# The output gate's vector of an encoder step: summed on ScalarE and GpSimd during the Q, K and V projections, instead of on TensorE inside the recurrent stage

## What is computed

```python
mod = jax.nn.silu(c) @ w_mod + b_mod                 # (1024) @ (1024, 3072)
shift, scale, gate = jnp.split(mod, 3, axis=-1)
hn = rms_norm(x, g_norm) * (1.0 + scale[:, None]) + shift[:, None]
u = hn @ w_in                                        # (T, 1024) @ (1024, 5192)
xa, za, q, k, v, zb, iq, ik, iw = jnp.split(u, IN_OFFSETS, axis=-1)
# A: causal conv of xa, then a gated linear recurrence over the positions (8 blocks of 128 channels)
ya = rms_norm(h.astype(dt), g_a) * jax.nn.silu(za)
# B: index scores pick the top keys of each query; softmax attention over them
yb = rms_norm(ob.astype(dt), g_b) * jax.nn.silu(zb)
y = jnp.concatenate([ya, yb], axis=-1) @ w_out
x_out = x + gate[:, None] * y
```

## Time and profile before

| | us |
|---|---|
| median of 3 runs | 1117.14 (1110.64 to 1118.58) |
| the profiled execution, its own time | 1114.59 |
| its span in the trace | 1112.8 |
| PE busy (5914 matmuls) | 1042.3, 94% |
| DVE busy | 839.2, 75% |
| ACT busy | 497.5, 45% |
| POOL busy | 380.3, 34% |

### The profile page before, as it was taken

One profiled execution on the slowest core, in us unless ns is written; L12 is line 12 of the kernel. 1 busy time (PEld: TensorE's weight loads), 2 busy tenths in 40 slices (PEclk: granted clock), 3 DMA queues, 4 the chain that ended last, 5 costly groups with the idle time before them and its releaser, 6 DMA issues.

```text
span 1112.8 us, 16575 instructions
## 1 busy us (share of the span) xinstructions
PE 1042.3 (94%) x5914; PEld 935.0 (84%) x5914; DVE 839.2 (75%) x1643; ACT 497.5 (45%) x827; POOL 380.3 (34%) x247
## 2 busy tenths in 40 slices
PE   6989898999999999999999997989899899999995
PEld 3679766799999999999999996778788778888873
DVE  1577699999998899999999995667766646543345
ACT  4432365421122677777764235566655524111111
POOL 0122366421111355555557462144231332212120
PEclk9989899999999999999999998999999999999998
DMA  9612001133234122222223432233331337233221
GB/s 298 198 43 67 19 1 40 40 99 96 79 99 109 55 81 81 81 81 69 76 77 101 153 122 87 62 90 96 95 95 29 96 95 236 59 112 100 80 67 57
DMA packets 128280, 100.78 MB, mean 91 GB/s; under 512 B 12176, under 2 KB 119200, under 8 KB 128224
## 3 DMA queue, kind: packets, MB, share of 16 engines
q1 hardware_dynamic: 128224, 100.04, 30.3%
HBM read 74.04 MB, written 25.99 MB: 90 GB/s over the span
## 4 chain that ended last, share of the span: by engine, by line
PE 56%; DVE 23%; issue 13%; ACT 4%; DMA 1%; SPq 1%; POOL 1%; DVEq 0%; ACTq 0%
PE ps L554 16%; PE ps L556 15%; PE ps L555 15%; DVE scores L1984 6%; PE ps L1704 5%; DVE best L1980 5%; DVE hidden L2028 2%; DVE conv L2006 2%; PE ps L1439 2%; DVE scores L1944 1%; PE ps L1424 1%; DVE mult L2023 1%; DMA q_raw<-q_scratch 1%; PE ps L1534 1%; DMA x_in<-in_x_prompt 1%
## 5 line engine op out<-in xcount | busy, mean ns | idle before, releaser
L554 PE MATMUL ps<-h_hi,w_hi 128*128 128x364 f32 (+1 forms) x984 | 327.1, 332 | 4.8 <-DVE h_lo L1882 4.1
L555 PE MATMUL ps<-h_lo,w_hi 128*128 128x364 f32 (+1 forms) x984 | 325.5, 331 | 0.0
L556 PE MATMUL ps<-h_hi,w_lo 128*128 128x364 f32 (+1 forms) x984 | 325.2, 331 | 0.0
L876 POOL TENSOR_TENSOR w_lo<-w_raw,w_hi 128x1024 fp32r<-128x1024 f32 (+1 forms) x41 | 101.2, 2470 | 317.5 <-ACT w_hi L1069 235.3
L554 PEld LDWEIGHTS ps<-h_hi,w_hi 128*128 128x128 f32 (+1 forms) x984 | 185.8, 189 | 6.5 <-issue 4.2
L555 PEld LDWEIGHTS ps<-h_lo,w_hi 128*128 128x128 f32 (+1 forms) x984 | 186.1, 189 | 1.5
L556 PEld LDWEIGHTS ps<-h_hi,w_lo 128*128 128x128 f32 (+1 forms) x984 | 185.4, 188 | 0.7
L1984 DVE MATCH_REPLACE8 scores<-best,scores 128x512 f32<-128x512 f32 (+6 forms) x204 | 172.3, 857 | 0.0
L1980 DVE MAX8 best<-scores 128x8 f32<-128x512 f32 (+6 forms) x204 | 162.8, 860 | 1.8
L1084 ACT ACTIVATE stage<-ps 128x364 f32<-128x364 f32 (+1 forms) x66 | 29.8, 475 | 141.6 <-PE ps L556 133.7
L988 POOL TENSOR_TENSOR y_lo<-y_raw,y_hi 128x1024 fp32r<-128x1024 f32 (+1 forms) x18 | 41.3, 2295 | 142.3 <-ACT y_hi L1341 142.3
(11 more groups left out here) (246 smaller groups left out, 2078.0 us busy)
## 6 DMA issues: line engine op xcount, KB each, us to landing
w_raw<-in_w_in SPq DMA_DIRECT2D x40, 512.0 KB, 4.6
w_mod_raw<-in_w_mod SPq DMA_DIRECT2D x8, 1024.0 KB, 12.6
y_raw<-y_scratch SPq DMA_DIRECT2D x16, 512.0 KB, 4.3
wo_raw<-in_w_out SPq DMA_DIRECT2D x10, 512.0 KB, 4.9
q_scratch<-stage SPq DMA_DIRECT2D x8, 546.0 KB, 3.6
y_scratch<-y_a SPq DMA_DIRECT2D x8, 546.0 KB, 3.5
zb_scratch<-stage SPq DMA_DIRECT2D x8, 546.0 KB, 4.1
x_in<-in_x_prompt SPq DMA_DIRECT2D x8, 512.0 KB, 8.2
```

The source lines that it names most:

```text
L554: nc.tensor.matmul(out, w_part_hi, x_hi, start=first, stop=False)
L555: nc.tensor.matmul(out, w_part_hi, x_lo, start=False, stop=False)
L556: return nc.tensor.matmul(out, w_part_lo, x_hi, start=False, stop=last)
L876: pool.tensor_tensor(w_lo[:, slot, :, 0:width], w_raw[:, slot, :, 0:width], f32(w_hi[:, slot, :, 0:width]), ALU.subtract).then_inc(w_lo_do ...
```

## The change

The last third of `w_mod` is summed elsewhere and earlier. ScalarE issues four loads of 1 MB behind the index stage. Behind each of eight sets of the Q, K and V projections it scales one block of rows by `silu(c)`, once for each of the two vectors, into `wg_part`; GpSimd adds this onto `wg_sum`. Between the first set of the recurrent stage and its loop, TensorE sums `wg_sum` over the partitions with 16 matmuls against a column of ones. The loads and the matmuls inside the loop go. `wg_raw` now has 1024 columns in each of its eight rows and lies over tiles of the recurrent stage, so ScalarE waits for the last add before that stage. The loops over the Q sets are written out on ScalarE and GpSimd.

```diff
-    wg_raw = z.take("wg_raw", [P, KT, P], F32)
+    wg_part = z.take("wg_part", [P, 2, D], F32)
+    wg_sum = z.take("wg_sum", [P, 2, D], F32)
+
+    wg_raw = at("wg_raw", [P, KT, D], F32, zone_x + 4 * nbytes([P, TP + 4], F32))
...
-            def load_gate_block(i):
-
-                if not isinstance(i, int) or i > 0:
-                    sp.wait_ge(gate_ready, i)
-                sp.dma_start(wg_raw[:, :, :], w_mod[:, :, bass.ds(i * P + 2 * D, P)]).then_inc(wg_in, 16)
...
+            def add_gate(k):
+
+                for b in range(2):
+                    pool.wait_ge(wg_scaled, 2 * k + b + 1)
+                    if k >= 1:
+                        pool.wait_ge(wg_added, 2 * k + b - 1)
+                        pool.tensor_tensor(wg_sum[:, b, :], wg_sum[:, b, :], wg_part[:, b, :], ALU.add).then_inc(wg_added, 1)
+                    else:
+                        pool.tensor_copy(wg_sum[:, b, :], wg_part[:, b, :]).then_inc(wg_added, 1)
...
+            def load_gate(n):
+
+                act.dma_start(wg_raw[:, 2 * n:2 * n + 2, :], w_mod[:, 2 * n:2 * n + 2, 2 * D:3 * D]).then_inc(wg_in[n], 16)
+
+            def scale_gate(k):
+
+                act.wait_ge(wg_in[k // 2], 16)
+                for b in range(2):
+                    if k >= 1:
+                        act.wait_ge(wg_added, 2 * k + b - 1)
+                    nc.scalar.activation(wg_part[:, b, :], wg_raw[:, k, :], ACT.Copy,
+                                         scale=silc[:, k, b:b + 1]).then_inc(wg_scaled, 1)
+
+            act.wait_ge(index_added, DVE_UNITS)
+            act.wait_ge(pool_added, 2 * POOL_UNITS)
+            act.wait_ge(index_ready, len(INDEX_UNITS))
+            for n in range(4):
+                load_gate(n)
...
                 split_w(j % 2, (j + 2) // 2 + 1, 3 * j + 3)
+                if m < 2:
+                    scale_gate(KT - 2 + m)
                 if m >= 1:
                     read_rows(m - 1)
             read_rows(3)
+            act.wait_ge(wg_added, 2 * KT)
...
             pe.wait_ge(kv_read, 12)
+            pe.wait_ge(wg_added, 2 * KT)
+            for m in range(KT):
+                for b in range(2):
+                    x = nc.tensor.matmul(ps[:, 7, 2 * m + b:2 * m + b + 1], wg_sum[:, b, P * m:P * (m + 1)], ones[:, 0:1],
+                                         start=True, stop=True)
+            x.then_inc(gate_ready, 1)
...
-
-                pe.wait_ge(wg_in, i * 16 + 16)
-                for k in range(KT):
-                    x = nc.tensor.matmul(ps[:, 7, bass.ds(i * 2, 2)], wg_raw[:, k, :], silc[:, k, :],
-                                         start=(k == 0), stop=(k == KT - 1))
-                x.then_inc(gate_ready, 1)
```

More of the change, by code:

```diff
@@ L476, in build @@
     gate_cols_done = sem("gate_cols_done")
-    wg_in = sem("wg_in")
+    wg_in = [sem(f"wg_in{i}") for i in range(4)]
+    wg_scaled = sem("wg_scaled")
+    wg_added = sem("wg_added")
     pad_edge = sem("pad_edge")
@@ L671, in store_ya @@
                 sp.dma_start(y_s[0, bass.ds(i, 1)].rearrange("h p t -> (h p) t"), y_a[:, :]).then_inc(ya_out, 16)
-            load_gate_block(0)
             load_w(J_LRU + 2, XA + P)
@@ L682, in lru_step @@
                 load_gates(i + 1)
-                load_gate_block(i + 1)
                 store_ya(i)
@@ L710, in load_values @@
                 sp.wait_ge(lru, 57)
-                sp.wait_ge(gate_ready, KT)
+                sp.wait_ge(gate_ready, 1)
                 sp.wait_ge(kv_out[0], 64)
@@ L905, in _ @@
                     pool.tensor_tensor(out, out, r, ALU.add).then_inc(pool_added, 1)
+            def add_gate(k):
[6 more added lines that the diff above has]
+                        pool.tensor_copy(wg_sum[:, b, :], wg_part[:, b, :]).then_inc(wg_added, 1)
             split_w(J_Q + 3, (J_Q + 1) % 2)
-            with pool.Fori(1, 4) as i:
-                for u in range(2):
-                    split_w(i * 2 + (J_Q + 2 + u), (J_Q + u) % 2)
-            for j in range(J_K + 2, J_LRU + 2):
+            for j in range(J_Q + 4, J_LRU + 2):
                 split_w(j, j % 2)
+                if j - (J_Q + 4) < KT:
+                    add_gate(j - (J_Q + 4))
             def split_gates(i):
@@ L1133, in _ @@
                         split_w(j % 2, (j + 2) // 2 + 1, 3 * j + 3)
-            read_set.parity = J_Q % 2
-            with act.Fori(1, 4) as i:
-                for u in range(2):
-                    slot = (J_Q + u) % 2
-                    act.wait_ge(staged[slot], i * 16)
-                    read_set(i * 2 + (J_Q + u), stage[:, slot, :], ACT.Copy)
-                    split_w(slot, i + ((J_Q + 2 + u) // 2 + 1), i * 6 + (3 * (J_Q + u) + 3))
+            def load_gate(n):
[12 more added lines that the diff above has]
+                load_gate(n)
+            read_set.parity = J_Q % 2
+            for j in range(J_Q + 2, J_K):
+                act.wait_ge(staged[j % 2], (j - J_Q) // 2 * 16)
+                read_set(j, stage[:, j % 2, :], ACT.Copy)
+                split_w(j % 2, (j + 2) // 2 + 1, 3 * j + 3)
+                scale_gate(j - (J_Q + 2))
             def read_rows(m):
@@ L2047, in _ @@
             n_select += PER_STEP * KT
-            dve.wait_ge(gate_ready, KT)
+            dve.wait_ge(gate_ready, 1)
             V.tensor_tensor(gate_cols[:, :, :], ps[:, 7, 0:16].rearrange("p (m b) -> p m b", b=2),
```

## The result

The changed kernel takes 1122.7 us (median of 16 runs, 1119.5 to 1125.2). The kernel before, run beside it, took 1115.0 (median of 16, 1110.6 to 1127.1). The ratio is 1.0061, with a 95% interval of 1.0044 to 1.0078. So it is slower by some 7 us and within 1%.

The account below looks back on a forecast made before the run. VectorE's list was taken to set the end from the first recurrent steps to attention, TensorE before; 0 + 3.5 + 2.0 - 1.7 = +3.8 us gave 1118.4 from the profiled 1114.59, 1120.9 from the median; stated 1120, range 1111 to 1128.

Parts of the forecast that it names:

- "+1 to +7": Whole kernel: VectorE leads and both additions on the path come through, +1 to +7 us; chance 0.68.
- The eight blocks for nothing: Recurrent loop: removing eight 1.71 us matmul blocks from TensorE gains 0, since VectorE's list covers them.
- The rival that TensorE sets the pace: Recurrent loop: TensorE leads, so the removed blocks bring 13.7 less 5.5, -8.2 us; chance 0.07.
- The block of 16 matmuls, +3.5: TensorE ahead of the loop: the new matmuls cost between 3.42 and 3.76 us, taken as +3.5.
- The scalings ahead of `read_rows`, +2.0: ScalarE behind the second K set: two scalings delay the row reads, leaving TensorE idle, +2.0 us.
- The copy in the last step, -1.7: VectorE, last step: GpSimd's weight split ends earlier, so the copy beside it waits 1.7 us less.
- other pairs may meet anew: Last step: VectorE's `mult` may lose 0.8 us, but new meetings with GpSimd are possible; left to the range.
- the fall behind the 3.5 us block: TensorE ahead of the loop: the clock could fall once at the new block, costing 1.5 us.
- The rival of a fall in each step: Loop: 1.7 us idle before the gates lowers TensorE's clock, up to 13.6 us, 1132; chance 0.12.
- At attention: Start of attention: VectorE's list sets it; TensorE's wait of 4.17 us stays about as long or grows.
- burst: Rival: four 1 MB loads delay a 512 KB weight load TensorE needs, +0 to 5 us; chance 0.08.
- The adds' rival: GpSimd's 16 adds slow VectorE's selection rounds beside them, +12 us on top, 1134; chance 0.05.

Follow-up runs that it names:

- run 5: Kernel before with the eight blocks and seven of eight loads left out of the loop, one block behind it: 1116.17 us, ratio 1.0022.
- run 7: Kernel before with VectorE relieved: selection rounds of tiles 3 and 2 dropped in each step: 1113.6 us, ratio 0.9977.
- run 1: Changed kernel with ScalarE reading the transposed rows before the scalings: 1120.44 us, ratio 1.0061 to the kernel before.
- run 6: Kernel before with the output gate's block of eight matmuls made twice in each step: 1145.37 us, ratio 1.0284.
- run 9: Changed kernel with two selection rounds of tiles 5 and 4 moved from behind the loop to ahead of it: 1120.56 us, ratio 1.0052.
- run 10: Changed kernel, rows read first, matmuls two per step, GpSimd's last square before its weight split, one selection round moved ahead of the loop: 1108.33 us.
- run 3: Changed kernel with rows read before the scalings and the 16 matmuls dealt out two to a step: 1115.01 us, ratio 1.0008.
- run 11: Kernel before with one selection round of tiles 5 and 4 moved from behind the loop to ahead of it: 1112.89 us, ratio 0.9982.
- run 2: Changed kernel with its 16 matmuls moved from ahead of the recurrent loop to behind it: 1121.67 us, ratio 1.0068.
- run 8: Changed kernel with VectorE relieved: selection rounds of tiles 3 and 2 dropped in each step: 1113.01 us, ratio 0.9988.

## Why the prediction was right, and where it wasn't

It said 1120 us, within 1% and slower by 3.8 in its sum; the time is 1122.7, within 1% and slower by 7. Nearly twice the step that was summed came. That 1120 still lies close to 1122.7 is in part luck: the forecast started from a median of 1117.14 of three runs, and sixteen runs give 1115.03. With 3.8 on top that would have been 1118.8. The measured difference, 6.7 us by the spans and 7.7 by the medians, stands at the upper end of what was bounded (+2.8 to +7.8) and, by the medians, outside the "+1 to +7" beside the chance of 0.68.

**The eight blocks for nothing:** right. Scans 28.90 us apart, TensorE's wait of 1.7 us before each step's gates, and run 5 without the blocks at the same pace. "Within a few tenths of a microsecond" turned out as 0.17 (run 7). The rival that TensorE sets the pace fell, if closely. The prediction said it would need VectorE's step to be 1.71 us shorter. That is the condition for the full gain; 0.2 us would already have let part of it in.

**The block of 16 matmuls, +3.5:** right in size, 3.63 in the changed kernel and 3.49 in run 1.

**The scalings ahead of `read_rows`, +2.0:** right for the stall, 2.07. That the clock might fall behind it was not thought of; it did in three of four profiles with this stall, for some 1.5 us more.

**The copy in the last step, -1.7:** this is the step that failed. The split moved against VectorE as was said: it began 1.30 us behind the scan's start before and 0.50 ahead of it after. But the working let it end sooner beside the same copy, and never asked what stands ahead of the copy. It is the scan, and the split now began before it. The copy gained 2.00 us and the scan lost 1.90. The term is about 0.

**What wasn't in the sum:** `k_lo` on VectorE, +1.80, the same kind of meeting some 60 us later. The prediction left such meetings to the range ("other pairs may meet anew"), which put no price on it. Both together, 1.6 + 1.8 = 3.4 us, are the difference between the +3.8 foreseen and the 6.7 read, less the 0.5 that came back behind attention.

**The clock:** the fall behind the 3.5 us block, put down as "1.5 us, once", came in the profiled execution (357.6 to 361.2), and the one of the earlier trace rows went, so the two cancel in this pair of executions. Over the gates, behind idle times of 1.7 us, the clock was 1.00 in the whole loop. The rival of a fall in each step is refuted for idle times of this size; it became true in run 6, behind 3.8 us of small matmuls.

**Adds and burst:** VectorE's rounds at 306.97 and 318.54 in the changed kernel are 11.57 us apart, as before. The weights next to the burst are rounded at 223.44, where the earlier trace rows has 223.33. Both rivals fell. The adds' rival was also summed too high: +12 on 1120 is 1132, not 1134.

**At attention:** the wait got longer (7.53), as said. That VectorE's list alone sets this start holds for 4.9 us of it (run 9); behind that, `norm_q` comes last.

## What to carry to other kernels

When two engines' lists are within a percent of each other, taking work from the shorter one is worth nothing here; shorten the longer list first (run 5: all blocks gone from TensorE's list, the same period; run 10: one round moved into an idle time of VectorE, 2.5 us less up to attention). Adding to the shorter list costs as soon as it becomes the longer (run 6). Work moved out of a covered loop must be put where it is covered too: in one block ahead of or behind the loop it cost 3.5 us and more, two matmuls a step in the loop's own wait left the period at 28.91 us (run 3).

When GpSimd and VectorE work side by side on element-wise operations with two inputs, ask for each meeting which one begins first; a shift of half a microsecond turned a saved wait into another here.

## What the hardware showed

**Where these operations of VectorE and GpSimd met, one ran after the other, and the first kept its pace.** In the changed kernel GpSimd's `k_lo` ends at 658.45 + 3.65 = 662.10 and VectorE's, begun in between, at 663.78, 1.68 us later; in run 11 it is 657.49 and 659.18, 1.69 later. VectorE's operation takes 1.82 alone, so it ran nearly as if it had started when GpSimd was done. The scan of the last step fits too: it ended at 606.20, 2.29 us behind the split's end (603.91), and takes 2.43 alone. The copy of the earlier trace rows too ended with the split beside it (598.68 + 2.17 = 600.85, and 597.51 + 3.31 = 600.82). The other way round, in the kernel before, VectorE's took 1.82, and GpSimd's 5.28 instead of 3.65. VectorE's MAX8 beside a split kept its 1.22. The Trainium skill (GPSIMD Engine Reference, Specifications) names contention between the two for VectorE's instructions with two inputs in SBUF; the trace agrees. In these meetings it wasn't a sharing at half speed but one after the other.

**The clock fell behind small matmuls though TensorE didn't pause in them.** Blocks of 3.5 to 4 us, 128 columns of weights against one or two moving columns, were followed by the lower clock in the changed kernel, in runs 2, 8 and 9 and in seven steps of run 6, and not in run 1. The granted clock of the next 3.4 to 3.6 us was 0.58 in the changed kernel and 0.52 in run 8. Blocks of 1.7 us weren't, in any of the seven steps whose period was read in the kernel before and in run 7. Each fall ahead of step 0 cost 1.5 us: from the third transposition of the second K set to ScalarE's rounding at 353 us it takes 44.69 us in the kernel before, where it fell, and 43.22 in run 1, where it didn't. Single idle times of 1.7 us in the loop, between dense stretches, had no such effect (granted clock 1.00 in the changed kernel from 370 to 600 us). Behind the stall of 3.19 us at the second K set it fell in three of four profiles.
